# Tokens first in the load queue, and eight projection strips interleaved with the filter products

## What is computed

```python
def first_block(x, ...):
    h = jnp.concatenate([meta, x], axis=1)
    a = rms_norm(h, norm_mix[l])
    p = a @ w_in[l]                                # 1024 -> 4096
    y_hy = hyena_mixer(p[..., :D_HYENA_PROJ], ...)  # 1536 columns: 12 strips of 128
    ...
    y_hg = hgrn2_mixer(p[..., D_HYENA_PROJ:], ...)  # 2560 columns: 20 strips
    h = h + jnp.concatenate([y_hy, y_hg], axis=-1) @ w_out[l]
    h = h + hier_moe(rms_norm(h, norm_ffn[l]), ...)

def hyena_filter_spectra(L, w1, b1, w2, b2, w3, freq):
    z = ...                                        # 33 positional features
    hid = jnp.sin(fr * (z @ w1 + b1))
    hid = jnp.sin(fr * (hid @ w2 + b2))
    filt = (hid @ w3).reshape(L, 2, HYENA_ORDER, D_HYENA) * window
    ...
    return jnp.fft.rfft(two_sided, axis=0)

def centred_short_conv(u, w, b):                   # 3 taps, on the 12 Hyena strips
    ...
```

## Time and profile before

| | us |
|---|---|
| median of three runs | 2566.71 |
| lowest and highest | 2566.13, 2588.36 |
| the profiled execution | 2564.53 |
| its span on the core | 2562.8 |
| TensorE busy, of the span | 2143.2 (84%) |
| VectorE busy, of the span | 911.7 (36%) |
| mean granted TensorE clock | 0.901 of full |

### The profile page before, as it was taken

How to read it: one execution, slowest core, us unless ns; L and a number is a source line. 1 busy time by engine, 2 the same in 40 slices (tenths; PEclk the granted TensorE clock), 3 DMA queues, 4 the chain that set the end, 5 groups by cost and what they waited for, 6 DMA issues and landing times. The chain is left out here.

```text
span 2562.8 us, 25793 instructions
## 1 busy us (share of the span) xinstructions
PE 2143.2 (84%) x10250; PEld 1416.8 (55%) x10250; DVE 911.7 (36%) x1500; ACT 290.7 (11%) x650; POOL 0.2 (0%) x4
## 2 busy tenths in 40 slices
PE   6997988667666666656666999999998999999998
PEld 3583466322222222223222777778887777868887
DVE  4245452211211111121121335455553235455553
ACT  1111021000000000000001222111002122111001
POOL 0000000000000000000000000000000000000000
PEclk7997777778888888888888999999999999999999
DMA  5130005799999999999997333324445333224442
GB/s 218 66 132 1 0 1 218 335 429 423 428 429 428 428 428 429 428 428 429 429 428 320 131 132 132 113 77 172 148 148 192 138 132 126 97 98 155 160 154 82
DMA packets 45198, 592.18 MB, mean 231 GB/s; under 512 B 5463, under 2 KB 6904, under 8 KB 7928
## 3 DMA queue, kind: packets, MB, share of 16 engines
q1 hardware_dynamic: 43672, 585.45, 56.7%
q10 hardware_dynamic: 1440, 5.57, 0.6%
HBM read 589.95 MB, written 1.05 MB: 231 GB/s over the span
## 5 line engine op out<-in xcount | busy, mean ns | idle before, releaser
L484 PE MATMUL ps<-arena,ring 128*128 128x256 f32 x1920 | 433.8, 382 | 7.9 <-DVE arena L911 7.8
L484 PEld LDWEIGHTS ps<-arena,ring 128*128 128x128 f32 x1920 | 362.4, 191 | 61.6 <-DVE arena L911 9.1
L1456 PE MATMUL ps<-ring,arena 128*32 128x512 f32 x2048 | 261.8, 658 | 111.9 <-DMA ring<-in_w_experts 92.1
L691 PE MATMUL ps<-arena,ring 128*128 128x256 f32 x1280 | 289.2, 378 | 0.0
L1470 PE MATMUL ps<-ring,arena 128*32 128x512 f32 x1024 | 179.0, 834 | 107.6 <-DMA ring<-in_w_experts 100.8
L691 PEld LDWEIGHTS ps<-arena,ring 128*128 128x128 f32 x1280 | 241.8, 189 | 35.3 <-issue 1.0
L1456 PEld LDWEIGHTS ps<-ring,arena 128*32 128x32 f32 x2048 | 65.0, 116 | 290.7 <-issue 148.2
L1470 PEld LDWEIGHTS ps<-ring,arena 128*32 128x32 f32 x1024 | 33.5, 133 | 236.6 <-DMA ring<-in_w_experts 156.9
L1250 PE MATMUL ps<-arena,ring 128*128 128x272 f32 (+1 forms) x640 | 150.6, 398 | 2.3 <-DVE arena L1731 2.3
L697 PE MATMUL ps<-arena,ring 128*128 128x256 f32 x640 | 151.6, 378 | 0.0
L1443 PE MATMUL ps<-arena 128*128 128x128 f32 x512 | 89.4, 356 | 67.2 <-DVE arena L1884 67.2
(11 more groups left out here) (347 smaller groups left out, 1802.7 us busy)
## 6 DMA issues: line engine op xcount, KB each, us to landing
ring<-in_w_experts SPq DMA_DIRECT2D x192, 2048.0 KB, 25.5
ring<-in_w_layers SPq DMA_DIRECT2D x44, 2048.0 KB, 7.8
ring<-in_w_layers SPq DMA_DIRECT2D x40, 1536.0 KB, 6.5
ring<-in_w_first SPq DMA_DIRECT2D x10, 2048.0 KB, 8.5
arena<-in_late ACTq DMA_DIRECT2D x2, 896.0 KB, 4.9
arena<-in_fourier SPq DMA_DIRECT2D x1, 1632.0 KB, 13.8
arena<-in_gm_rows ACTq DMA_DIRECT2D x2, 768.0 KB, 6.3
arena<-in_const SPq DMA_DIRECT2D x1, 1141.0 KB, 5.2
```

Source lines behind the costliest of these rows:

```text
L484: last = pe.matmul(ps[:, j % 2, 0:SEQ], t[:, s, k, :], lhs[:, k, :], start=(k == 0), stop=(k == KD - 1))
L691: last = pe.matmul(ps[:, j % 2, 0:SEQ], t[:, k, :], an[:, k, :], start=(k == 0), stop=(k == KD - 1))
L1456: last = pe.matmul(ps[CAP * e:CAP * (e + 1), v // 4, :], xg[:, (v % 4) * 2 + k, CAP * e:CAP * (e + 1)], w[:, k, e, :], start=(v % 4 == 0 a ...
```

## The change

SP now issues the tokens `h` first, then constants, block-one parameters, features, two filter weights and unit 0 of the projection weights; the third filter weight and the window follow unit 0, and positions, layer-two parameters and Fourier matrices follow unit 1. TensorE does the norm sum ahead of the first filter layer, strip 0 between the first and the second filter layer, strips 1 to 3 between the second layer and the filter products, and strips 4 to 7 between filter products and spectrum products. ScalarE and VectorE follow this order. The operations themselves, their shapes and their number are the same.

```diff
+LEAD = 8
@@ sync
+            sp.dma_start(xr(h), d["h"]).then_inc(sem("in_h"), 16)
             sp.dma_start(const, d["const"]).then_inc(sem("in_const"), 16)
             sp.dma_start(param1, d["param1"]).then_inc(sem("in_param1"), 16)
-            for l in range(LAYERS):
-                sp.dma_start(param2[:, l * w_param2:(l + 1) * w_param2], d["param2"][l]).then_inc(sem("in_param2"), 16)
-            sp.dma_start(pos_i[:, :], d["positions"].partition_broadcast(P)).then_inc(sem("in_pos"), 16)
             sp.dma_start(feat[0:33, 0:T], d["features"][0:33, 0:T]).then_inc(sem("in_feat"), 16)
             sp.dma_start(fw1[0:33, :], d["filt_w1"]).then_inc(sem("in_feat"), 16)
             sp.dma_start(fw2[0:64, :], d["filt_w2"]).then_inc(sem("in_feat"), 16)
-            sp.dma_start(xr(h), d["h"]).then_inc(sem("in_h"), 16)
-            sp.dma_start(fw3[0:64, :, :], ...).then_inc(sem("in_w3"), 16)
-            sp.dma_start(xr(window), ...).then_inc(sem("in_w3"), 16)
-            sp.dma_start(four.rearrange("p a b c -> p (a b c)"), d["fourier"]).then_inc(sem("in_four"), 16)
             for u in range(10):
                 if u >= RING1:
                     sp.wait_ge(sem("strip"), 4 * (u - RING1 + 1))
                 sp.dma_start(ring[:, u % RING1, :], d["w_first"][u]).then_inc(sem(f"w1_in{u % RING1}"), 16)
+                if u == 0:
+                    sp.dma_start(fw3[0:64, :, :], ...).then_inc(sem("in_w3"), 16)
+                    sp.dma_start(xr(window), ...).then_inc(sem("in_w3"), 16)
+                if u == 1:
+                    sp.dma_start(pos_i[:, :], d["positions"].partition_broadcast(P)).then_inc(sem("in_pos"), 16)
+                    for l in range(LAYERS):
+                        sp.dma_start(param2[:, l * w_param2:(l + 1) * w_param2], d["param2"][l]).then_inc(sem("in_param2"), 16)
+                    sp.dma_start(four.rearrange("p a b c -> p (a b c)"), d["fourier"]).then_inc(sem("in_four"), 16)
@@ tensor
-            pe.wait_ge(sem("in_feat"), 48)
-            pe.matmul(ps[0:64, 2, 0:T], fw1[0:33, :], zT[0:33, :], start=True, stop=True).then_inc(sem("hid"), 1)
-
             pe.wait_ge(sem("sq_mix"), 1)
             pe.wait_ge(sem("in_const"), 16)
             norm_sum(pe, ones, a, KD, ps[:, 3, 0:T], sem("ss_mix"))
+            pe.wait_ge(sem("in_feat"), 48)
+            pe.matmul(ps[0:64, 2, 0:T], fw1[0:33, :], zT[0:33, :], start=True, stop=True).then_inc(sem("hid"), 1)
+            pe.wait_ge(sem("normed_mix"), KD)
+            strip(0, 0, 0, lambda k: a[:, k, :], T)
             pe.wait_ge(sem("hid_act"), 1)
             pe.matmul(ps[0:64, 2, 0:T], fw2[0:64, :], hid[0:64, :], start=True, stop=True).then_inc(sem("hid"), 1)
+            for j in range(1, 4):
+                strip(j, j // 4, j % 4, lambda k: a[:, k, :], T)
             pe.wait_ge(sem("hid_act"), 2)
             pe.wait_ge(sem("in_w3"), 32)
...
-            pe.wait_ge(sem("normed_mix"), KD)
-            for j in range(4):
+            for j in range(4, LEAD):
                 strip(j, j // 4, j % 4, lambda k: a[:, k, :], T)
             pe.wait_ge(sem("in_four"), 16)
             pe.wait_ge(sem("filt_sd"), 4)
...
-            for j in range(4, HY + HG):
+            for j in range(LEAD, HY + HG):
                 strip(j, j // 4, j % 4, lambda k: a[:, k, :], T)
@@ scalar
-            for i in range(2):
-                act.wait_ge(sem("hid_arg"), i + 1)
-                act.activation(hid[0:64, :], hid[0:64, :], ACT.Sin).then_inc(sem("hid_act"), 1)
+            act.wait_ge(sem("hid_arg"), 1)
+            act.activation(hid[0:64, :], hid[0:64, :], ACT.Sin).then_inc(sem("hid_act"), 1)

             for j in range(HY + HG):
-                if j == 4:
+                if j == 1:
+                    act.wait_ge(sem("hid_arg"), 2)
+                    act.activation(hid[0:64, :], hid[0:64, :], ACT.Sin).then_inc(sem("hid_act"), 1)
+                if j == LEAD:
                     for n in range(12):
...
@@ vector
             dve.wait_ge(sem("in_param1"), 16)
+            dve.wait_ge(sem("rstd_mix"), 1)
+            dve.wait_ge(sem("ss_mix"), 1)
+            for k in range(KD):
+                dve.scalar_tensor_tensor(a[:, k, :], h[:, k, :], P1("norm_mix", k), rstd, ALU.mult, ALU.mult).then_inc(sem("normed_mix"), 1)
             for i in range(2):
                 dve.wait_ge(sem("hid"), i + 1)
...
+            for j in range(4):
+                short_conv(j)
             dve.wait_ge(sem("in_w3"), 32)
...
+            for j in range(4, LEAD):
+                short_conv(j)
             dve.wait_ge(sem("in_pos"), 16)
...
-            for j in range(HY + HG):
+            for j in range(LEAD, HY + HG):
```

More of the change, by code:

```diff
@@ L1209, in _ @@
             sp.dma_start(fw2[0:64, :], d["filt_w2"]).then_inc(sem("in_feat"), 16)
-            sp.dma_start(xr(h), d["h"]).then_inc(sem("in_h"), 16)
-            sp.dma_start(fw3[0:64, :, :], d["filt_w3"].rearrange("k (a b) -> k a b", b=HALF)).then_inc(sem("in_w3"), 16)
-            sp.dma_start(xr(window), d["features"][:, T:T + 3 * HALF]).then_inc(sem("in_w3"), 16)
-            sp.dma_start(four.rearrange("p a b c -> p (a b c)"), d["fourier"]).then_inc(sem("in_four"), 16)
             for u in range(10):
@@ L1217, in _ @@
                 sp.dma_start(ring[:, u % RING1, :], d["w_first"][u]).then_inc(sem(f"w1_in{u % RING1}"), 16)
+                if u == 0:
+                    sp.dma_start(fw3[0:64, :, :], d["filt_w3"].rearrange("k (a b) -> k a b", b=HALF)).then_inc(sem("in_w3"), 16)
+                    sp.dma_start(xr(window), d["features"][:, T:T + 3 * HALF]).then_inc(sem("in_w3"), 16)
+                if u == 1:
[3 more added lines that the diff above has]
+                    sp.dma_start(four.rearrange("p a b c -> p (a b c)"), d["fourier"]).then_inc(sem("in_four"), 16)
             def expert_unit(v, g, free):
@@ L1605, in _, with short_conv @@
             dve.memset(padded[:, :, T + 1:T + 2], 0.0).then_inc(sem("edges"), 1)
+            def short_conv(j):
+                job_evacuated(dve, j)
+                src = padded[:, j % 4, :]
+                y = conv[:, j, :]
+                link(dve.tensor_scalar(y, src[:, 0:T], P1("conv_w", j), P1("conv_b", j), ALU.mult, ALU.add))
+                link(dve.scalar_tensor_tensor(y, src[:, 1:T + 1], P1("conv_w", HY + j), y, ALU.mult, ALU.add))
+                dve.scalar_tensor_tensor(y, src[:, 2:T + 2], P1("conv_w", 2 * HY + j), y, ALU.mult, ALU.add).then_inc(sem("convolved"), 1)
+                if j < 4:
+                    dve.wait_ge(sem("convolved"), j + 1)
+                    dve.nop().then_inc(sem("z"), 1)
             dve.wait_ge(sem("in_param1"), 16)
+            dve.wait_ge(sem("rstd_mix"), 1)
+            dve.wait_ge(sem("ss_mix"), 1)
+            for k in range(KD):
+                dve.scalar_tensor_tensor(a[:, k, :], h[:, k, :], P1("norm_mix", k), rstd, ALU.mult, ALU.mult).then_inc(sem("normed_mix"), 1)
             for i in range(2):
```

## The result

The changed kernel takes 2545.82 us (median of four runs, 2542.83 to 2549.08). The kernel before, run beside it again, has a median of 2574.93 us (four runs, 2566.13 to 2588.36), and the ratio is 0.987 with a 95% interval of 0.983 to 0.991: 1.3% faster. The time is 2 us from the 2548 that I predicted, and inside the range. The forecast of the change against before failed: I forecast 0.7%, with a chance of 0.94 that it would lie within 1% of no change. Both halves have their reason, and they are different ones.

A forecast was written before the change was run, and what follows sets the result against it. TensorE bounds the first part from 48.5 us on, the start-up chain before. Gains of 5.5 (earlier `a`), 10.5 (filter products at full clock) and 2.4 (second sine hidden) make 18.4 us: 2548 us predicted, range 2542 to 2559.

The forecast's parts named there:

- The start: TensorE's row up to strip work: tokens at 6.0 us, norm sum from 9.0, strip 0 at 19.2; gain 18.4 us.
- The clock in the filter products: Twelve filter products behind dense strips run at full clock, 10.5 us instead of 20.95; gain 10.5 us.
- rival one: Filter products lose the clock again: 2556 us, or 2560 at half clock from the first product; chance 0.13.
- Unit 0: Weights for strip 0 land at 15.5 us, so their load is hidden with 3.7 us to spare.
- rival two: Unit 0 lands at 28 us because loads of one queue share engines: 8.7 us lost, 2557; chance 0.05.
- The 2.2 us paid in both kernels: Strip 0, after a rest of TensorE, costs 5.84 us against 3.68 for a later strip, before and after the change.
- Cover: VectorE's sums and differences lie under strips 4 to 7, ending at about 56 us, before the spectrum products want them.
- Past that point everything is as before, only earlier: Work after the start and spectrum products only moves earlier; the DMA-bound expert loop moves along and absorbs nothing.
- rival three: Convolution and scan change their clock: 268 to 291 us runs at half, 21.6 us lost, 2570 us; chance 0.03.
- its mirror: The stretch from 204 to 268 us runs at full clock, up to 18 us gained, 2530 us; chance 0.04.
- The rule weighed: Throttled by default, released by activity: filter products behind dense strips at full clock; strip 0, after a rest, charged 5.84 us.

The follow-up runs named there:

- loads-only kernel: The kernel before with the change's order of loads alone, every engine's order as before; median 2577.79 us, ten runs in two groups.
- warm start: The change plus unread products, three ahead of the norm sum and seven between first filter layer and strip 0; median 2559.64 us.
- LEAD = 4 kernel: The change with strips 4 to 7 left behind the spectrum products, everything else as in the change; 2560.10 us (2558.7 to 2565.3).

## Why the prediction was right and wrong, point by point

**The start: right.** Tokens used at 5.79 (6.0 in the sum), norm sum at 8.78, released by the constants (9.0), strip 0 at 19.14 (19.2), filter products at 36.55 (36.5) and 10.6 us long (10.5), strips 4 to 7 at 47.17 (47.0), the first transpose behind the last strip at 185.24 (about 185). Its gain of 18.4 is 17.9 in the profiles, 19.75 between the two kernels whose clock is held.

**The clock in the filter products: right, rival one fell.** This window of the changed kernel is on them:

```profile
36.55:47.17 10.62, 10.62 (x26) 3.57 (x25) 8.62 (x14) 0.39 (x1) 0.00 (x0) 1.00 0.55 204
```

The same products that stayed at 0.50 for 21 us in before and in the loads-only kernel stayed at 1.00 here: in both cases the clock was the one at which TensorE had come to them.

**Unit 0: right, rival two fell.** Strip 0 waited for VectorE, even in the kernel where unit 0 stands last in the queue. The Trainium skill, DMA: Bandwidth & Descriptors, HWDGE ordering, says that on each DMA engine descriptors are consumed in ring order, though not that loads complete in that order. This case agrees as far as unit 0, last in the queue, had landed by 26.85 us, when strip 0 started.

**The 2.2 us paid in both kernels: right for the sum, short for what it is worth.** Strip 0 and norm sum together take 11.4 to 13.2 us in the two profiles of the changed kernel, and 8.06 in the warm start's, 3 to 5 us less.

**Cover: right, and never priced.** I wrote of strips 4 to 7 only that VectorE's work lies under them. Without them 9.0 us of wait and 7.3 us of half clock appear, 16 in all.

**"Past that point everything is as before, only earlier": this is the step that failed.** The instructions are the same, their duration isn't: the stretch from the first transpose to the output projection took 185.3 or 205.7 us in before and 184.0 and 181.1 in the changed kernel. I had the mechanism as rival three and gave it and its mirror 0.07 together, on two grounds. The one, that the sequence of operations is the same, is true and says nothing. The other, that two of three runs agree within 0.6 us, left out the third, 22 us above: a run of the upper group, as 70 of the 105 are. Rival three also aimed at the change, not at before, and at the wrong stretch: its 21.6 us were those of 268 to 291 us, which kept full clock in the upper execution, while 16 of the 20.4 us arose behind it. That the two sizes are alike is chance.

What I took for the time of before was its lower group, a third of its runs; the forecast of 0.7% hangs on it. The changed kernel has its convolution where none of ten runs lost the 20 us. That was luck: nothing in the change was made for it, and with 1.7 us more work the median is 2567 against 2583. The time came out as forecast because I had started from a lower-group execution, and the changed kernel has only that group. The 18.4 us of the start were worked out; that no run of the changed kernel lost the 20 us was not. Why a kernel comes to one place more often than to another stays open.

**The rule weighed.** The Trainium skill, TensorE: Matmul & The Clock Gate, Part 1, has throttled as the default and activity releasing it. The runs agree with the fall in rests, and with the return 3.3 to 5.1 us into the first strips. The rule alone doesn't cover the rest: 21 us of 64-row filter products back to back ran at half clock to their end, the spectrum products of the LEAD = 4 kernel for 15 us, and the upper execution of before was at half for 27 us over two convolution blocks with a rest of 4.0 us between them; there the measurement decides.

## What to carry to other kernels

Look at all runs of the kernel before, not at its median, and ask for a cause when one of three is 0.8% off: if the profile shows a stretch at mixed clocks, the time of that stretch can be a lottery whose odds any edit ahead of it changes, and an edit's ratio then measures the odds as well as the work. To tell them apart, add a microsecond or two of dead work ahead of the stretch in both kernels, or hold the clock in both. Here, short rests of TensorE on another engine, 2 to 4 us each and harmless in the list of waits, cost most by what the clock did behind them, and dead products in a free PSUM bank were a cheap cure: 57 of them took 18 us off.

## What the runs showed of the hardware that I had not expected

- The same 549 matmul records took 181.1 to 205.7 us, depending on where they fell against the clock's changes; places 0.2 us apart, in two kernels, went with 181.1 and 201.0 us.
- Adding 1.3 us of work made a kernel 18 us faster at the median, and adding 114 matmul records to a stretch made it 15.5 us shorter.
- The clock came back 3.3 to 5.1 us into the first strips (twelve profiles), 15 us into the spectrum products of the LEAD = 4 kernel, and not at all in the 21 us of filter products in before.
- The tokens, behind small loads in the queue, were used at 12.4, 13.3, 13.4, 14.9 and 15.3 us in five profiles; first in the queue, at 5.8 to 5.9 us in nine.
